# Turning the prompt's rows ahead of the samples', and the first product ahead of the squares, at the start of a decoder step

## The reference

```python
def rms_norm(x, g):
    y = xf * lax.rsqrt(jnp.mean(xf * xf, axis=-1, keepdims=True) + EPS)
    return (y * g).astype(x.dtype)

hn = rms_norm(h, g_pre[i])
proj = hn @ w_in                                   # q, k, v, g and 16 low-rank gate columns
gk = log_sigmoid(proj[..., i4:] @ w_gk2 + b_gk) / GATE_NORM
```

## Time and profile before

| what | before |
|---|---|
| time of the runs, median of 3 | 873.5 us (872.85 to 874.04) |
| time of the profiled execution | 875.32 us |
| its span, first to last instruction | 873.6 us |
| TensorE busy | 819.9 us, 94% |
| VectorE busy | 566.1 us, 65% |
| ScalarE busy | 482.1 us, 55% |
| GpSimd busy | 348.3 us, 40% |
| mean DMA rate over the span | 271 GB/s |
| rate of the first 60 us | 362 GB/s |
| mean granted TensorE clock | 0.989 |

### The profile page before, as it was taken

One profiled execution on the slowest core, in us unless ns is written; L12 is line 12 of the kernel. 1 busy time (PEld: TensorE's weight loads), 2 busy tenths in 40 slices (PEclk: granted clock), 3 DMA queues, 4 the chain that ended last, 5 costly groups with the idle time before them and its releaser, 6 DMA issues.

```text
span 873.6 us, 14850 instructions
## 1 busy us (share of the span) xinstructions
PE 819.9 (94%) x5001; PEld 573.1 (66%) x5001; DVE 566.1 (65%) x620; ACT 482.1 (55%) x1603; POOL 348.3 (40%) x211
## 2 busy tenths in 40 slices
PE   5999999988999999999999999999979997999995
PEld 3666667766754434444478878777745544899995
DVE  4545375788976777887898654332178996655553
ACT  4611382235676677769986433312288895444433
POOL 3000000966685998686895000000166763011110
PEclk9999999999999999999999999999979999999998
DMA  9999868645689997997998089998887989521302
GB/s 327 380 372 334 320 223 292 218 144 203 219 293 357 395 341 242 332 322 272 395 381 319 1 326 339 365 323 311 309 319 278 333 324 377 210 97 49 98 1 98
DMA packets 109820, 236.79 MB, mean 271 GB/s; under 512 B 7505, under 2 KB 66712, under 8 KB 109488
## 3 DMA queue, kind: packets, MB, share of 16 engines
q1 hardware_dynamic: 51136, 174.29, 54.7%
q10 hardware_dynamic: 58608, 61.54, 21.1%
HBM read 222.54 MB, written 13.27 MB: 270 GB/s over the span
## 4 chain that ended last, share of the span: by engine, by line
PE 55%; DVE 14%; ACT 11%; DMA 10%; issue 4%; POOL 3%; SPq 2%; ACTq 0%; POOLq 0%; DVEq 0%
PE ps L1759 19%; PE ps L1762 8%; PE ps L1746 7%; PE ps L2196 5%; PE ps L1743 4%; DMA slot<-in_cache_k_dram 4%; ACT slot L907 4%; DVE w_lo L1216 2%; PE ps L1723 2%; DMA work<-in_cache_v_dram 2%; POOL slot L641 2%; DMA w_raw<-in_gla_w_in_dram 2%; DVE zall L1402 2%; DVE states L1436 2%; DVE slot L1401 1%
## 5 line engine op out<-in xcount | busy, mean ns | idle before, releaser
L641 POOL TENSOR_TENSOR slot<-slot,qb 128x1024 f32<-128x1024 f32 x97 | 252.4, 2633 | 100.5 <-DMA slot<-in_cache_k_dram 63.0
L1402 DVE TENSOR_REDUCE zall<-slot 128x16 f32<-128x1024 f32 x97 | 116.9, 1215 | 28.1 <-POOL slot L641 27.0
L1216 DVE TENSOR_TENSOR w_lo<-w_raw,w_hi 128x1024 fp32r<-128x1024 f32 x57 | 82.2, 1443 | 78.5 <-ACT w_hi L736 78.3
L907 ACT ACTIVATE slot<-slot 128x64 f32<-128x64 f32 x496 | 119.3, 244 | 18.9 <-POOL slot L641 18.9
L736 ACT CAST w_hi<-w_raw 128x1024 fp32r<-128x1024 f32 x58 | 60.7, 1047 | 73.7 <-PE ps L1762 36.8
L907 ACT ACTIVATION_READ_ACCUMULATOR slot<-slot 128x1 f32 x496 | 94.3, 190 | 0.0
L1746 PE MATMUL ps<-xn,w_raw 128*128 128x512 f32 x192 | 85.4, 596 | 1.7 <-ACT xn L747 1.7
L1746 PE MATMUL ps<-xn,w_unsplit 128*128 128x512 f32 x192 | 83.7, 593 | 0.0
L1762 PE MATMUL ps<-xa_hi,w_hi 128*128 128x512 f32 x200 | 81.7, 409 | 1.7 <-DVE w_lo L1216 1.7
L1759 PE MATMUL ps<-xb_hi,w_hi 128*128 128x260 f32 x384 | 78.9, 287 | 1.1 <-DVE w_lo L1216 0.9
L1762 PE MATMUL ps<-xa_hi,w_lo 128*128 128x512 f32 x200 | 79.2, 396 | 0.0
(11 more groups left out here) (326 smaller groups left out, 1508.0 us busy)
## 6 DMA issues: line engine op xcount, KB each, us to landing
slot<-in_cache_k_dram SPq DMA_DIRECT2D x128, 512.0 KB, 6.2
slot<-in_cache_v_dram SPq DMA_DIRECT2D x120, 512.0 KB, 6.0
w_raw<-in_gla_w_in_dram ACTq DMA_DIRECT2D x12, 1024.0 KB, 7.3
slot<-in_gla_w_in_dram SPq DMA_DIRECT2D x24, 512.0 KB, 9.5
w_raw<-in_w_kv_dram ACTq DMA_DIRECT2D x8, 1024.0 KB, 11.2
w_raw<-in_w_ple_gate_dram ACTq DMA_DIRECT2D x6, 1024.0 KB, 5.3
s<-in_state_gla_dram SPq DMA_DIRECT2D x1, 4096.0 KB, 22.3
out_dram<-s ACTq DMA_DIRECT2D x4, 1024.0 KB, 8.7
```

Source lines behind the costliest of these rows:

```text
L641: nc.gpsimd.tensor_tensor(slot[s][:], slot[s][:], qb[:, (n // NPG) % 2, :], ALU.mult).then_inc(S("k_mul_pool"), 1)
L907: ins = nc.scalar.activation(part, part, ACT.Copy, accum_out=zall[:, n % NPG, b * SH + h:b * SH + h + 1])
L1216: nc.vector.tensor_tensor(lo, raw, hi.bitcast(F32), ALU.subtract).then_inc(S("w_split"), 1)
L1402: nc.vector.tensor_reduce(zall[:, n % NPG, b * SH:(b + 1) * SH], at.rearrange("p (h d) -> p h d", d=HD), AX.X, ALU.add).then_inc(S("k_used ...
```

## The change

ScalarE: a Sqrt of a scratch column ahead of the wait for the vectors loads that function's table early; the gain column is copied as before. The samples' squares and their root move from ahead of the prompt's tiles to behind tiles 0 and 2, the split of weight block 0 moves from behind tile 7 to behind tile 5, and the four bias copies move behind the samples' Ln. The split of block 1 now comes before the copy of the partial squares.

VectorE: the samples' stationary operand is made behind tile 2, the low part of block 0 behind tile 6, the samples' reciprocal after the last tile.

TensorE: prompt tiles 0 and 1 are turned first, then the samples' rows, then the other tiles; `s_rows` of blocks 0 and 1 come behind tile 4 (before: behind tiles 3 and 4). The first product comes right behind the low-rank columns, ahead of the second half of the squares, of blocks 5 to 7 and of the whole squares. The bias broadcasts move behind the wait for `s_lrt`, and the wait for their copies to just ahead of the samples' g rows.

```diff
@@ -800,30 +800,35 @@
             act.dma_start(wgk[:, :, :], gla_w_in[0].rearrange("(k p) n -> p k n", p=P)[:, :, 3072:3072 + RANK]).then_inc(S("wgk_in"), 16)
             load_pair(1)
             act.wait_ge(S("consts"), 1)
+            nc.scalar.activation(ytok[:, 5:6], epsc[:], ACT.Sqrt)
             act.wait_ge(S("gcol_t"), 1)
             nc.scalar.copy(gcol[:], bank[7][:, 0:NVEC]).then_inc(S("gcol"), 1)
-            act.wait_ge(S("xs_in"), 16 * 5)
-            s_square(0, xs[:])
-            act.wait_ge(S("bias_mm"), 1)
-            s_root(0, sC[:, 320:321], D)
-            nc.scalar.copy(biasbc[:], sC[:, 416:416 + SH])
-            nc.scalar.activation(nbiasbc[:], sC[:, 416:416 + SH], ACT.Copy, scale=-1.0)
-            nc.scalar.copy(biascol[:], sC[:, 432:433])
-            nc.scalar.activation(nbiascol[:], sC[:, 432:433], ACT.Copy, scale=-1.0).then_inc(S("bias_out"), 1)
+            act.wait_ge(S("gcol"), 1)
 
             for k in range(KT):
                 act.wait_ge(S("x_T"), k + 1)
                 x_hi(k, hT[:, k, 0:NP_TOK])
                 square(k, hT[:, k, 0:NP_TOK])
-            split_hi(0)
+                if k == 0:
+                    act.wait_ge(S("xs_in"), 16 * 5)
+                    s_square(0, xs[:])
+                if k == 2:
+                    act.wait_ge(S("s_fold"), 1)
+                    s_root(0, sC[:, 320:321], D)
+                if k == 5:
+                    split_hi(0)
+            split_hi(1)
             partial_squares(0)
-            split_hi(1)
             rms(0)
             split_hi(2)
             act.wait_ge(S("s_dz"), 1)
             own.then(nc.scalar.activation(deS[:], dzS[:], ACT.Abs))
             own.then(nc.scalar.activation(deS[:], deS[:], ACT.Exp, scale=-1.0))
             nc.scalar.activation(deS[:], deS[:], ACT.Ln, bias=1.0).then_inc(S("s_ln"), 1)
+            nc.scalar.copy(biasbc[:], sC[:, 416:416 + SH])
+            nc.scalar.activation(nbiasbc[:], sC[:, 416:416 + SH], ACT.Copy, scale=-1.0)
+            nc.scalar.copy(biascol[:], sC[:, 432:433])
+            nc.scalar.activation(nbiascol[:], sC[:, 432:433], ACT.Copy, scale=-1.0).then_inc(S("bias_out"), 1)
             split_hi(3)
             act.wait_ge(S("s_dz"), 2)
             nc.scalar.activation(deS[:], dzS[:], ACT.Exp, scale=1 / GATE_NORM).then_inc(S("s_dec"), 1)
@@ -1258,19 +1263,21 @@
             dve.wait_ge(S("bias_in"), 16)
             nc.vector.tensor_copy(biasrow[0:1, SH:P].rearrange("o (b h) -> o b h", h=SH),
                                   biasrow[0:1, 0:SH].unsqueeze(1).to_broadcast([1, NS - 1, SH])).then_inc(S("rows_set"), 1)
-            dve.wait_ge(S("gcol"), 1)
-            dve.wait_ge(S("s_t"), 1)
-            s_stationary(hsA, 0)
-            nc.vector.tensor_copy(pTs[:], sB[:, HV:HV + 2 * SW].rearrange("p (c t) -> p c t", c=2)).then_inc(S("s_p"), 1)
-            s_recip(0)
-
             for k in range(KT):
                 dve.wait_ge(S("xt"), k + 1)
                 nc.vector.tensor_copy(hT[:, k, 0:NP_TOK], bank[4 + k % 3]).then_inc(S("x_T"), 1)
+                if k == 0:
+                    dve.wait_ge(S("gcol"), 1)
                 if k:
                     x_lo(k - 1, hT[:, k - 1, 0:NP_TOK])
+                if k == 2:
+                    dve.wait_ge(S("s_t"), 1)
+                    s_stationary(hsA, 0)
+                    nc.vector.tensor_copy(pTs[:], sB[:, HV:HV + 2 * SW].rearrange("p (c t) -> p c t", c=2)).then_inc(S("s_p"), 1)
+                if k == 6:
+                    split_lo(0)
             x_lo(KT - 1, hT[:, KT - 1, 0:NP_TOK])
-            split_lo(0)
+            s_recip(0)
             split_lo(1)
             dve.wait_ge(S("s_lr"), 1)
             nc.vector.tensor_scalar(lrS[:], sB[0:SW, 336:336 + RANK], srstd[0:SW, 0:1], None, ALU.mult).then_inc(S("s_qk"), 1)
@@ -1849,16 +1856,7 @@
                     last = nc.tensor.transpose(bank[4][:, b * P:(b + 1) * P], src[:, b * P:(b + 1) * P], ident[:])
                 last.then_inc(done, 1)
 
-            pe.wait_ge(S("xs_in"), 16 * 5)
-            for c in range(2):
-                nc.tensor.transpose(sB[:, HV + c * SW:HV + (c + 1) * SW], psS[:, c * P:(c + 1) * P], ident[0:SW, 0:SW])
-            s_transposed(xs)
-            s_sum(1)
-            pe.wait_ge(S("rows_set"), 3)
-            nc.tensor.matmul(sC[:, 416:416 + SH], ones[0:1, :], biasrow[0:1, 0:SH], start=True, stop=True)
-            nc.tensor.matmul(sC[:, 432:433], biasrow[0:1, :], ones[0:1, 0:1], start=True, stop=True).then_inc(S("bias_mm"), 1)
             pe.wait_ge(S("x_in0"), 16)
-            pe.wait_ge(S("gcol"), 1)
             for k in range(KT):
                 if k == KT // 2:
                     pe.wait_ge(S("x_in1"), 16)
@@ -1867,12 +1865,20 @@
                 for b in range(TB):
                     last = nc.tensor.transpose(bank[4 + k % 3][:, b * P:(b + 1) * P], xin[:, b, k * P:(k + 1) * P], ident[:])
                 last.then_inc(S("xt"), 1)
+                if k == 1:
+                    pe.wait_ge(S("xs_in"), 16 * 5)
+                    for c in range(2):
+                        nc.tensor.transpose(sB[:, HV + c * SW:HV + (c + 1) * SW], psS[:, c * P:(c + 1) * P], ident[0:SW, 0:SW])
+                    s_transposed(xs)
+                if k == 2:
+                    s_sum(1)
                 if k == 5:
                     square_parts(0, 0)
-                if k == 3:
+                if k == 4:
                     pe.wait_ge(S("s_hs"), 1)
-                    pe.wait_ge(S("bias_out"), 1)
-                if k >= 3:
+                    pe.wait_ge(S("s_sqrt"), 1)
+                    s_rows("qk", hsA, 0, KT)
+                if k >= 4:
                     s_rows("qk", hsA, k - 3, KT)
             pe.wait_ge(S("s_p"), 1)
             pe.wait_ge(S("wgk_in"), 16)
@@ -1880,17 +1886,20 @@
                 last = nc.tensor.matmul(sB[0:SW, 336:336 + RANK], hsA[:, k % SV, SW * (k // SV):SW * (k // SV + 1)], wgk[:, k, :],
                                         start=(k == 0), stop=(k == KT - 1))
             last.then_inc(S("s_lr"), 1)
+            product(0, 0, wait_x=True)
             square_parts(0, 1)
             for k in range(KT - 3, KT):
                 s_rows("qk", hsA, k, KT)
             square_whole(0)
-            product(0, 0, wait_x=True)
 
             pe.wait_ge(S("s_qk"), 3)
             nc.tensor.transpose(sB[:, 0:P], qkS[:, 0:P], ident[:])
             nc.tensor.transpose(sB[0:RANK, 352:352 + SW], lrS[:], ident[0:SW, 0:SW]).then_inc(S("s_t"), 1)
             pe.wait_ge(S("s_lrt"), 1)
             pe.wait_ge(S("w2_in"), 16)
+            pe.wait_ge(S("rows_set"), 3)
+            nc.tensor.matmul(sC[:, 416:416 + SH], ones[0:1, :], biasrow[0:1, 0:SH], start=True, stop=True)
+            nc.tensor.matmul(sC[:, 432:433], biasrow[0:1, :], ones[0:1, 0:1], start=True, stop=True)
             for h in range(GH):
                 last = nc.tensor.matmul(sC[:, 384 + h * NS:384 + (h + 1) * NS], w2[:, h * P:(h + 1) * P], lrT[:, 0:NS],
                                         start=True, stop=True)
@@ -1938,6 +1947,7 @@
                     s_attend(b)
                     s_outer(b + 2)
             pe.wait_ge(S("s_dz"), 1)
+            pe.wait_ge(S("bias_out"), 1)
             s_rows("g", hsA)
             product(PHASES["k"][0], 0)
             for b in (4, 5):
```

## The result

The changed kernel took 877.8 us (median of 11 runs, 875.6 to 880.6) against 874.0 for the kernel before on the same chip (872.9 to 877.9): ratio 1.0037, with an interval of 1.0023 to 1.0051 (it is not simply the quotient of the two medians, which differ by 3.8 us). It is slower, by 3.2 us with an interval of 2.0 to 4.5, and lies above the predicted range of 872.0 to 876.8. Over all 51 runs of it the median is 876.6, over all 138 of the kernel before 874.15: 2.45 us. The first measurement was on the high side, but the sign stands.

A forecast was written before the change was run, and what follows sets the result against it. TensorE, busy 94% of the span, was taken as the bound: 0.15 us ahead at the v blocks, 1.6 lost to the clock, part swallowed by a later wait, left +0.7, so 874.2 us; range 872.0 to 876.8.

The forecast's parts named there:

- Turning first, the product's start, the chain: At the start: tiles turned from 8.1, first product at 21.1, then 12.9 us to the low-rank matmuls, TensorE idle 3 us.
- The bias matmuls: Moved behind the low-rank rows' wait, they cost some 0.5 us at full clock, leaving the v blocks 0.15 us ahead.
- The clock: In the new hole TensorE's clock falls for 3.4 us, costing the v blocks 1.6 us.
- The DMAs that move: Blocks 13 to 15 and the samples' state, issued later behind a saturated queue, cost nothing, or up to 1 us.
- further down: At the 68.55 wait: 1.45 us late at the v blocks, up to 0.9 swallowed, +0.7 left.
- What the wait swallows: TensorE's 0.93 us wait at 68.55 for a weight pair absorbs up to 0.9 us of lateness.
- The sum: At the v blocks -0.15 + 1.6 = 1.45 us late; after the wait swallows its part, +0.7.
- slower: Rival, chance 0.20: clock rises late, product starts at 22.9, clock falls in the hole; +2.35 us, 875.9.
- Clock doesn't fall: Rival, chance 0.20: TensorE's clock stays up in the hole; -0.15 us at the v blocks is kept, 873.4.
- Faster: Rival, chance 0.12: the 4.2 us lead reaches the v blocks, TensorE not waiting for the norm's chain; 869.3.
- Change does little: Rival, chance 0.03: the samples' DMA still holds TensorE before tile 0; some us longer, partly swallowed, within the bound.

The follow-up runs named there:

- a1: The changed kernel measured again unchanged, first repeat; ratio 1.0031 to the kernel before.
- a2: The changed kernel measured again unchanged, second repeat; ratio 1.0028 to the kernel before.
- e3: The changed kernel with three unused 512-column matmuls put where TensorE waits for the low-rank rows; 876.5 us, ratio 1.0033.
- e1: The changed kernel with only the first product put back behind the whole squares; 875.3 us, ratio 1.0006.
- e4: The changed kernel with the samples' eight v blocks run ahead of the wait for the low-rank rows; 874.9 us, ratio 1.0003.
- e2: The kernel before with only the first product moved ahead of the second squares; 885.1 us, ratio 1.0114.
- e6: The kernel before with the third weight pair issued as soon as its buffer is free; 873.2 us, ratio 0.999.
- e9: e1 with the bias matmuls back among the first tiles and the third weight pair issued early; 875.8 us, ratio 1.0009.
- e12: The kernel before with the third weight pair issued early and the v blocks ahead of the low-rank rows' wait; 871.4 us, ratio 0.9968.
- e5: The changed kernel with the first quarter of the samples' state (1 MB) issued ahead of weight block 13; 875.3 us, ratio 1.001.
- a3: The changed kernel measured again unchanged, third repeat; ratio 1.0023 to the kernel before.
- a4: The changed kernel measured again unchanged, fourth repeat; ratio 1.0017 to the kernel before.
- e8: The changed kernel with the two bias broadcasts alone put back among the first tiles; 877.9 us, ratio 1.004.
- e10: The changed kernel with 24 extra unused identity matmuls on TensorE from about 2 us; 878.3 us, ratio 1.0048.

## Why the prediction was wrong

Step by step, in its own order.

**Turning first, the product's start, the chain: right.** Tiles from 8.34 (8.1), one table load ahead at 5.51 with the gain copy behind at 8.44, the product at 21.18 (21.1) in the early way and at 22.15 (upper end 22.9) in the late one. From the product to the next work of TensorE 33.90 - 21.18 = 12.7 (12.9), the hole 3.30 (3), with the copy behind the evacuation as what TensorE waited for. The table load cost what the row of before had: Exp started 1.30 us after it (32.41 against 31.11), 1.29 in the earlier trace rows, now with nothing beside the chain.

**The bias matmuls: 0.4 too little at times.** 0.88 us (33.90 to 34.78) and not 0.5 in the first profile, where the clock was down already; 0.47 in a1.

**The clock: right in kind, undersized in three profiles of five.** It stood at 0.50 for 6.8 us there, where I had taken one stretch of 3.4. In the first profile the loss is 0.41 on the bias matmuls (0.88 against 0.47 in a1), 0.80 on the low-rank ones (1.78 against 0.98) and 1.29 on the v blocks (36.56 to 41.44, against 35.65 to 39.24), 2.5 us and not 1.6. Where it stood for 3.4 us, in a1, the v blocks took 5.28 against 3.59, 1.7 more: there the term's size holds. Its 1.02 us for a block is the start's figure, and no run shows that the slow start is the level of 0.50, since the column reads 1.00 there; what the runs show is a v block every 0.85 us at 0.50 and every 0.43 at 1.00 (a1, by the starts of the matmuls). That the hole brings it down was an inference from the earlier trace rows. It fits the first profile and a2, where the fall began inside the hole, but it isn't the whole cause: with the hole filled (e3) or gone (e1) the clock fell as well, for 3.4 us, and with the v blocks in it (e4) it didn't. The cause stays open. In e1 and e3 TensorE stood no longer than 0.70 and 0.53 us at a time in the twelve before the fall, and their rows don't bear the inference out as I had used it.

**The DMAs that move: the step that failed.** I wrote "nothing, or up to 1 us", took nothing, and gave as the reason that block 12 lands only at 31.0, so that the queue is saturated to there. The landing of a transfer didn't say that all sixteen engines had work up to then. In e2 block 12 landed at 30.9, and in the two microseconds from 29 on the engines had been busy 0.19 and 0.02 of the time, with 74 and 8 GB/s. The trace after shows 303 GB/s where there were 412: at 27 to 35 us bytes for 1.04 us are missing, in the late way (a2) for 2.0; the pair was 1.22 and 2.50 late. And the second half of the step was that lateness of a transfer not wanted before 35.5 costs nothing. It costs in full here, where the front of the kernel is bound by bytes (362 GB/s over the first 60 us before, 356 after): the pair on which the g blocks depend lands when about 23 MB have been moved since the start (22.8 before, 22.9 after and in e1, 23.0 in e3 and e2), whether it was issued at 46.40, 48.59, 47.16, 47.73 or 55.50, and within 0.4 us of the last of the samples' eight g blocks (63.03 and 63.20 before, 64.25 and 63.90 after). That holds in all the profiles in which at least five of these blocks were issued ahead of it. Where it was issued ahead of most of them (e4, e6, e9, e12) it landed with 18.8 to 21.8 MB moved, 4 to 11 us before the last, and in e4 a dry queue cost it nothing. So the second half of *further down*, too, is wrong: I had the pair's lateness hang on its issue, part of which the wait would swallow. Behind the full queue it hung on what the queue had missed thirty microseconds earlier, 1.22 us late for 1.04 us of bytes and 2.50 for 2.0 in a2, and nothing swallowed that. e5 shows it: with the queue fed and the hole and the fall left alone, the pair was in time although it was issued 1.46 later than before, and the g blocks were 0.41 late, about what the rest of my sum gives (0.7).

**What the wait swallows: right in size, beside the point.** TensorE's path had 1.05 us of slack (I took 0.9) and was 2.20 late: 1.15 would have been left. The transfer was 1.22 late. By chance the two are nearly the same in the first profile; in a1 and a3 only the transfer is late by that much (1.21 and 1.82 against 0.10 and 0.66), in a4 it is TensorE.

**The sum.** I had +0.7 at the g blocks. They are +1.2 in the first profile and +1.2 to +2.5 in five, mean 1.74: that is 1 us of the miss. The rival *slower* had the late start, priced it at 2.35, and gave 875.9; a2 has nearly that, +2.51, but by the transfers. I had it as a case apart with a chance of 0.20, whereas early and late starts are mixed in the executions of one kernel, and the early ones lose transfers too. Of the 2.45 us measured, 1.74 is there at the g blocks. Some 0.7 isn't accounted for: from 519 to 618 us the mean lateness of the five profiles is 1.3 to 1.7, at their end 1.35, so it isn't seen to grow there; the single runs of one kernel scatter over 7 us, and falls of the clock further down come and go, so it may be chance. It stays open. The median of before, which I had at 873.5 from three runs, is 874.15 in 138, another 0.6 of the distance to the figure; and 877.8 was itself 1.2 above the median of all 51 runs, which is chance.

**The range** ended at 876.8 because I had added 0.9 for a dry queue once, on top of the slower rival. The first measurement, 877.8, is above; the four others (875.7 to 876.5) are inside it and above the forecast.

**The other rivals.** *Clock doesn't fall*: it fell in all five. *Faster*: the norm's chain was what TensorE waited for, and that rival fell with the row at 33.90. *Change does little*: the tiles were turned at once.

## What to carry to other kernels

A long piece of work, moved here ahead of the short ones which free the DMA's slots, stopped the transfers (0 GB/s from 31 to 35 us in e2, 303 instead of 412 from 27 to 31 in the changed kernel); look at the rate in the stretch where the moved piece will run, count the bytes that are in flight, and if the stage behind is bound by bytes, charge every missed byte to the transfer that is issued last. Ask of the transfer that the next wait hangs on how much is issued ahead of it: behind at least five of eight blocks the pair paid for the gap (+1.22 after, +2.50 in a2), ahead of most of them it didn't (-0.83 in e4, with 249 GB/s). Before moving a producer earlier, see what its consumer waits for besides; here the cheap move was the one that put ready work (the v blocks) ahead of a wait, and the early turning only shifted the idle time.

## What the runs showed of the hardware that I had not expected

- Issued behind at least five of eight 512 KB loads of the other queue, between 45.8 and 55.5 us, a 1 MB pair landed within 0.4 us of the last of them, with 22.6 to 23.1 MB moved since the start, whatever its issue time. Issued behind one or two of them (e4, e6, e9, e12) it landed 4 to 11 us before the last.
- The granted clock fell to 0.50 for 3.4 us in e1 and e3 with no wait of TensorE over 0.7 us in the twelve before it, behind 1.4 us of matmuls with 1 and 16 rows; it did not in e4 and e12, where the v blocks came straight behind the turned rows. That the small matmuls are the cause was not shown, and they are not needed: in the first profile, a2, e2, e8 and e10 it fell inside the hole of 2.4 to 3.3 us ahead of them, each time for 6.8 us.
- At the start eight turns take 1.97 us at 8.34 and 1.07 at 12.22 in one execution, 1.95 at 12.45 in another, while the column of the granted clock reads 1.00; with matmuls from 2 us on they take 1.09 at 9.32. That column does not show the slow start.
